# Attention with the transposes two steps and the value products three steps behind the scores, and the sink as a column of the score tile

## The chip, the cores and the metric

The kernel runs on 1 core of a Trainium2 chip. The metric is the device time of one execution in microseconds (us). The core's engines work in parallel, each on its own instruction queue: TensorE (PE, with its weight loads as PEld), VectorE (DVE), ScalarE (ACT), GpSimd (POOL) and SyncE (SP), which issues the loads of weights. They wait for each other by semaphores.

## The reference

Two blocks in a row on 512 tokens of width 1024. The first (a pooling mixer and a gated linear recurrence) isn't touched by the change. The second has two layers, each of this form:

```python
h = jnp.einsum('bsd,de->bse', x, w_in[l]) + b_in[l]
q, k, v, z_a, u_g, v_g, z_g, g_a, g_g = split_columns(h)
y_a = sliding_window_attention(q, k, v, attn_sinks[l]) * silu(z_a)
y_g = chunked_spatial_gating(gelu(u_g), gelu(v_g), ...) * silu(z_g)
merged = sigmoid(g_a) * (y_a @ w_branch_attn[l]) + sigmoid(g_g) * (y_g @ w_branch_gmlp[l])
x = layer_norm(ALPHA * x + merged @ w_out[l] + b_out[l], ln_g[l], ln_b[l])
...
# sliding_window_attention: 8 query heads, 2 key heads of 64, blocks of 128, window 128
scores = scores - slopes[:, :, None, None] * dist
scores = jnp.where(valid, scores, -jnp.inf)
m = jnp.maximum(scores.max(-1, keepdims=True), sink)
p = jnp.exp(scores - m)
denom = p.sum(-1, keepdims=True) + jnp.exp(sink - m)
out = (p / denom) @ v
```

A block of 128 queries sees its own block of 128 keys and the one before it. Block 0 sees only its own.

## The kernel before, in words

All matrix products with weights are made of three matmuls (`products`, L363 to L365): the weights and the activations are split into a part hi and a rest lo, and hi x hi, hi x lo and lo x hi are added up in PSUM. A *unit* is one output tile of 128 rows by 512 tokens: 8 contraction tiles of three matmuls, 24 in all. Its accumulator is `acc[0]` or `acc[1]` in turn, so a unit starts only when the result of the unit two before it has been evicted (`acc_done`).

The weights come in by SyncE to `raw`. In the second block VectorE makes `whi` of a piece (`c_split`, the CAST L1887) and GpSimd then makes `wlo` (`split_lo`, L358: `raw` less `whi`, both in SBUF), three units ahead of TensorE's use.

The order of the second block is written out in a list, `C_ORDER`. Its units are q0 to q3, k, v, za0 to za3, u0 to u3, vg0 to vg3 (one quarter of the contraction each, over all of `acc`), zg0 to zg3, ga0 to ga3, gg0 to gg3, then the branch products, and gates and branches again for the other half. Each engine walks this list; its part of an entry is its *slot*. ScalarE evicts a unit or makes its sigmoid or Gelu; for za and zg VectorE multiplies the sigmoid with the unit and so evicts it (L1896). After vg3 VectorE adds the bias (L1904), ScalarE does the Gelu (L1464), and VectorE takes mean and variance in the slot of zg0 (`vg_norm`, L1866 to L1873), of which ScalarE takes the root (L1467) before it makes the sigmoid of zg1. `vg_scale` (L1879) follows in the slot of zg1, and GpSimd multiplies and adds the norm's weights (L895, L897) behind its `split_lo` in four slots from zg3 on.

Hung to these units is the attention. A step is a head pair `p` and a block `b` of 128 queries, 16 steps a layer, one to each unit from za1 on (`side.append(("att", att))`). TensorE does its part of a step behind the unit, and VectorE and ScalarE behind the eviction. In slot s this happens:

- TensorE: scores of step s into the one bank `aux[:, 0]` (L1056, once the scores of step s-1 have been read), transposes of the probabilities of step s-1 (L1066), products with v of step s-2 (L1078).
- VectorE, `att_vector`: distance and mask added (L1814), maximum (L1818), maximum with the sink, its negation, and sink less maximum (L1821 to L1824). Then `c_split` of a weight piece. Then `att_vector_norm`: sum of exponentials and sink (L1832), reciprocal (L1834), scaling of the probabilities (L1837), and for the last block of a head pair the product of the output with za and its rest (L1842, L1845).
- ScalarE, `att_scalar`: the exponentials with their sum (L1376), exponential of the sink (L1379); then `att_scalar_turned`: the turned probabilities of step s-1 to SBUF (L1386), and the output's part hi (L1392).

The tiles `sc`, `pr`, `pt` and `sm` have two buffers each, by the step's parity.

## Time and profile before

| | before |
|---|---|
| time, median of 3 runs | 1731.24 us (1730.32 to 1731.7) |
| the profiled execution | 1731.74 us, span 1729.9 us |
| mean granted clock of TensorE | 0.987 of full |
| busy share of PE, DVE, ACT, POOL | 95%, 60%, 32%, 23% |
| attention of layer 0, first scores to last products | 1056.3 to 1196.4 us |
| the same of layer 1 | 1412.9 to 1554.1 us |

Times within the span count from its start. The durations used are those of the one profiled execution. An idle time is one of an engine between two of its instructions, put down to the instruction that ended it. Matmuls overlap their neighbours in the records, so the pace of TensorE is read from start to start.

### The profile page before, as it was taken

How to read it: one execution, taken by the hardware profiler on the slowest of the kernel's cores; microseconds unless marked ns; L12 is line 12 of the kernel's file. 1: busy time of each engine (PE TensorE's matmuls, PEld its weight loads, DVE VectorE, ACT ScalarE, POOL GpSimd, SP SyncE). 2: the span in 40 equal slices, each digit the busy share in tenths (PEclk: the TensorE clock that was granted, in tenths of full speed). 3: DMA queues.
4: the chain of work that ended last, by engine and by line, in shares of the span. 5: the costliest groups of instructions: out<-in, count | busy, mean ns of one | idle time of the engine just before them, and what ended most of it. 6: DMA issues, size and time to landing. Idle time of an engine off the chain costs nothing.

```text
span 1729.9 us, 31676 instructions
## 1 busy us (share of the span) xinstructions
PE 1643.8 (95%) x12890; PEld 1422.3 (82%) x12890; DVE 1042.3 (60%) x1636; ACT 555.5 (32%) x1000; POOL 393.1 (23%) x345
## 2 busy tenths in 40 slices
PE   7999899999999999999999799989999999989998
PEld 6999899988888888788887697757887887668876
DVE  6757475745765667476574366676525756664446
ACT  4323231333243232324323235453112235441121
POOL 0000000000422224042242123325350043253410
PEclk9999999999999999999999899999999999999999
DMA  3332223213212222221221132212223332222231
GB/s 128 98 94 89 67 96 98 93 55 103 74 51 74 75 68 81 73 65 60 74 75 62 49 121 86 73 49 98 73 98 122 112 92 71 73 66 81 98 122 49
DMA packets 112625, 142.23 MB, mean 82 GB/s; under 512 B 3068, under 2 KB 88480, under 8 KB 112480
## 3 DMA queue, kind: packets, MB, share of 16 engines
q1 hardware_dynamic: 108368, 133.07, 23.3%
q10 hardware_dynamic: 4032, 6.89, 1.3%
q8 instruction: 107, 1.75, 0.4%
q14 instruction: 38, 0.31, 0.1%
q0 software_dynamic: 80, 0.20, 0.0%
HBM read 137.01 MB, written 2.10 MB: 80 GB/s over the span
## 4 chain that ended last, share of the span: by engine, by line
PE 81%; DVE 11%; ACT 5%; issue 2%; DMA 0%; POOL 0%; DVEq 0%; SPq 0%; ACTq 0%; POOLq 0%
PE acc L363 23%; PE acc L365 22%; PE acc L364 22%; PE aux L517 2%; DVE sm L1832 1%; PE aux L363 1%; PE aux L365 1%; PE aux L364 1%; PE aux L534 1%; ACT pr L1376 1%; DVE ab L584 1%; PE aux L544 1%; PE aux L542 1%; DVE qb L573 1%; PE aux L503 1%
## 5 line engine op out<-in xcount | busy, mean ns | idle before, releaser
L363 PE MATMUL acc<-xhi,whi 128*128 128x264 f32 (+2 forms) x1888 | 632.4, 335 | 12.0 <-issue 4.4
L364 PE MATMUL acc<-xlo,whi 128*128 128x264 f32 (+2 forms) x1888 | 617.8, 327 | 0.0
L365 PE MATMUL acc<-xhi,wlo 128*128 128x264 f32 (+2 forms) x1888 | 617.5, 327 | 0.0
L363 PEld LDWEIGHTS acc<-xhi,whi 128*128 128x128 f32 x1888 | 357.0, 189 | 50.5 <-issue 13.0
L365 PEld LDWEIGHTS acc<-xhi,wlo 128*128 128x128 f32 x1888 | 357.4, 189 | 30.7
L364 PEld LDWEIGHTS acc<-xlo,whi 128*128 128x128 f32 x1888 | 357.6, 189 | 28.3 <-issue 0.9
L358 POOL TENSOR_TENSOR wlo<-raw,whi 128x1024 fp32r<-128x1024 f32 x84 | 205.0, 2441 | 352.5 <-DVE whi L1887 352.5
L354 ACT ACTIVATE whi<-raw 128x1024 fp32r<-128x1024 f32 x160 | 165.8, 1048 | 169.2 <-PE acc L365 156.7
L1680 DVE TENSOR_TENSOR wlo<-raw,whi 128x1024 fp32r<-128x1024 f32 x77 | 93.8, 1221 | 68.6 <-ACT whi L354 68.6
L358 DVE TENSOR_TENSOR wlo<-raw,whi 128x1024 fp32r<-128x1024 f32 x83 | 101.0, 1221 | 42.5 <-ACT whi L354 42.5
L1887 DVE CAST whi<-raw 128x1024 fp32r<-128x1024 f32 x84 | 65.7, 784 | 73.0 <-PE acc L365 73.0
L873 POOL TENSOR_TENSOR kb<-kb,tb 128x264 f32<-128x264 f32 (+1 forms) x96 | 85.5, 891 | 67.3 <-PE aux L517 36.0
L873 POOL TENSOR_TENSOR kb<-kb,fb 128x264 f32<-128x264 f32 x16 | 15.7, 980 | 363.4 <-PE aux L517 363.4
L859 POOL MEMSET ab<- 128x512 f32 x2 | 1.0, 526 | 375.1 <-DVE xlo L401 375.1
L363 PE MATMUL acc<-zhia,whi 128*128 128x264 f32 x256 | 73.6, 288 | 6.1 <-DVE zloa L1620 6.1
L573 DVE TENSOR_TENSOR qb<-qb,tb 128x256 f32<-128x256 f32 x96 | 64.9, 676 | 13.5 <-PE aux L517 8.9
L365 PE MATMUL acc<-zhia,wlo 128*128 128x264 f32 x256 | 72.7, 284 | 0.0
L364 PE MATMUL acc<-zloa,whi 128*128 128x264 f32 x256 | 72.6, 284 | 0.0
L1832 DVE TENSOR_TENSOR sm<-sm 128x2 f32<-128x2 f32 x32 | 58.1, 1816 | 21.3 <-ACT sm L1379 21.3
L1376 ACT ACTIVATE pr<-sc,sm 128x256 f32<-128x256 f32 (+1 forms) x64 | 30.4, 475 | 74.3 <-DVE sm L1824 74.3
L363 PEld LDWEIGHTS acc<-zhia,whi 128*128 128x128 f32 x256 | 48.1, 188 | 7.3 <-DVE zloa L1620 6.9
L1614 DVE TENSOR_TENSOR h<-acc,h 128x528 f32<-128x528 f32 x32 | 22.6, 708 | 51.0 <-PE acc L365 51.0
(282 smaller groups left out, 2755.6 us busy)
## 6 DMA issues: line engine op xcount, KB each, us to landing
raw<-in_w_in SPq DMA_DIRECT2D x38, 1024.0 KB, 5.1
raw<-in_hgrn_w_in SPq DMA_DIRECT2D x32, 1024.0 KB, 5.4
raw<-in_pool_w_in SPq DMA_DIRECT2D x16, 1024.0 KB, 5.2
raw<-in_pool_w_out SPq DMA_DIRECT2D x8, 1024.0 KB, 4.9
raw<-in_hgrn_w_out SPq DMA_DIRECT2D x8, 1024.0 KB, 5.0
raw<-in_w_out SPq DMA_DIRECT2D x8, 1024.0 KB, 4.9
raw<-in_pool_w_grp SPq DMA_DIRECT2D x4, 1024.0 KB, 5.3
raw<-in_w_branch_attn SPq DMA_DIRECT2D x4, 1024.0 KB, 5.0
```

The source lines that it names most:

```text
L354: act.activation(piece(whi, kind, m), raw_view(kind, m), ACT.Copy).then_inc(hi_ready, 1)
L358: dve.tensor_tensor(piece(wlo, kind, m), raw_view(kind, m), piece(whi, kind, m), ALU.subtract).then_inc(lo_ready, 1)
L363: pe.matmul(dst, stat[0], mov[0], start=first, stop=False)
L364: pe.matmul(dst, stat[0], mov[1], start=False, stop=False)
L365: return pe.matmul(dst, stat[1], mov[0], start=False, stop=last)
L517: mm = pe.matmul(dst, keys, q, start=True, stop=True)
L573: dve.tensor_tensor(second_halves(q, m), second_halves(q, m), blocks.unsqueeze(2).to_broadcast([P, CH * nb, m]), ALU.mult)\
L873: pool.tensor_tensor(first_halves(k, m), first_halves(k, m), both[:, :, 1].unsqueeze(2).to_broadcast([P, n, m]), ALU.mult)\
L1376: act.activation(pr[z][:, x, lo:], sc[z][:, x, lo:], ACT.Exp, bias=sm[z][:, 2, x:x + 1], accum_out=sm[z][:, 4, x:x + 1])\
L1680: dve.tensor_tensor(piece(wlo, kind, m), raw_view(kind, m), piece(whi, kind, m), ALU.subtract).then_inc(lo_ready, 1)
L1832: dve.tensor_tensor(sm[z][:, 6, :], sm[z][:, 4, :], sm[z][:, 5, :], ALU.add).then_inc(aprob, 1)
L1887: dve.tensor_copy(piece(whi, kind, M), raw_view(kind, M)).then_inc(hi_ready, 1)
```

## The change

The same work is put in another order and the sink is taken in otherwise. The transposes of a step stand two slots behind its scores, and the products with v three slots; the list gets one more slot for it (ga3). VectorE's sum, reciprocal and scaling move from behind the weight split of slot s to the start of the attention part of slot s+1 (in `att_vector`), ahead of the masking of step s+1's scores. The output of a head pair (`att_vector_out`) comes one slot later. ScalarE copies the turned probabilities ahead of the exponentials and no longer behind them. `sc` and `pr` get 257 columns, the last of which is the sink: it is copied in where a head pair begins (for either buffer), maximum, exponential and sum run over it, and so the separate operations on the sink fall out. The reduction gives the maximum negated.

```diff
-            sc = [sb(f"sc{s}", [P, 2, 2 * P], where=before_m) for s in range(2)]
-            pr = [sb(f"pr{s}", [P, 2, 2 * P], where=before_m) for s in range(2)]
+            sc = [sb(f"sc{s}", [P, 2, 2 * P + 1], where=before_m) for s in range(2)]
+            pr = [sb(f"pr{s}", [P, 2, 2 * P + 1], where=before_m) for s in range(2)]
...
-                    elif att < len(ATT) + 2 and att >= len(ATT):
+                    elif att < len(ATT) + 3 and att >= len(ATT):
...
-                if 1 <= s <= len(ATT):
-
-                    b = ATT[s - 1][1]
-                    pe.wait_ge(aprob, 4 * (base + s - 1) + 4)
-                    pe.wait_ge(apt_ready, 1 + base + s - 1)
+                if 2 <= s < len(ATT) + 2:
+
+                    t = s - 2
+                    b = ATT[t][1]
+                    pe.wait_ge(aprob, 3 * (base + t) + 3)
+                    pe.wait_ge(apt_ready, 1 + base + t)
                     for x in range(2):
                         for kb_ in range(0 if b else 1, 2):
                             mm = pe.transpose(aux2[:, 0, P * (2 * x + kb_):P * (2 * x + kb_ + 1)],
-                                              pr[(s - 1) % 2][:, x, P * kb_:P * kb_ + P], ident[:, :])
+                                              pr[t % 2][:, x, P * kb_:P * kb_ + P], ident[:, :])
                     mm.then_inc(apt_full, 1)
-                if 2 <= s:
-
-                    p, b = ATT[s - 2]
-                    pe.wait_ge(apt_ready, 1 + base + s - 1)
+                if 3 <= s:
+
+                    t = s - 3
+                    p, b = ATT[t]
+                    pe.wait_ge(apt_ready, 1 + base + t + 1)
                     if b == 0:
                         pe.wait_ge(ya_ready, 1 + 4 * i + p)
...
-                                           pt[(s - 2) % 2][:, 2 * x + kb_, :],
+                                           pt[t % 2][:, 2 * x + kb_, :],
...
             def att_scalar(i, s):
                 base = 16 * i
-                if s < len(ATT):
-                    p, b = ATT[s]
-                    lo, z = (0 if b else P), s % 2
-                    act.wait_ge(arow, 4 * (base + s) + 4)
-                    for x in range(2):
-                        act.activation(pr[z][:, x, lo:], sc[z][:, x, lo:], ACT.Exp,
-                                       bias=sm[z][:, 2, x:x + 1], accum_out=sm[z][:, 4, x:x + 1])\
-                           .then_inc(aexp, 1)
-                    act.activation(sm[z][:, 5, :], sm[z][:, 3, :], ACT.Exp).then_inc(aexp, 1)
-
-            def att_scalar_turned(i, s):
-                if 1 <= s <= len(ATT):
-                    b = ATT[s - 1][1]
-                    act.wait_ge(apt_full, 16 * i + s)
-                    z, first = (s - 1) % 2, (0 if b else 1)
+                if 2 <= s < len(ATT) + 2:
+                    t = s - 2
+                    z, first = t % 2, (0 if ATT[t][1] else 1)
+                    act.wait_ge(apt_full, base + t + 1)
                     act.activation(pt[z][:, :, :].rearrange("p (x k) q -> p x k q", x=2)[:, :, first:, :],
                                    aux2[:, 0, :].rearrange("p (x k q) -> p x k q", x=2, k=2)[:, :, first:, :],
                                    ACT.Copy).then_inc(apt_ready, 1)
-                if s >= 2 and ATT[s - 2][1] == CH - 1:
-                    p = ATT[s - 2][0]
+                if s < len(ATT):
+                    lo, z = (0 if ATT[s][1] else P), s % 2
+                    act.wait_ge(arow, base + s + 1)
+                    for x in range(2):
+                        act.activation(pr[z][:, x, lo:], sc[z][:, x, lo:], ACT.Exp,
+                                       bias=sm[z][:, 0, x:x + 1], accum_out=sm[z][:, 1, x:x + 1])\
+                           .then_inc(aexp, 1)
+                if s >= 3 and ATT[s - 3][1] == CH - 1:
+                    p = ATT[s - 3][0]
                     act.wait_ge(ya_ready, 1 + 4 * i + p + 1)
                     act.activation(yah[:, p, :], sq[p % 2][:, 0:SEQ], ACT.Copy).then_inc(yahi_ready, 1)
...
-                    for what, s in side:
-                        if what == "att":
-                            att_scalar_turned(i, s)
...
             def att_vector(i, s):
                 base = 16 * i
+                if 1 <= s < len(ATT) + 1:
+                    t = s - 1
+                    lo, z = (0 if ATT[t][1] else P), t % 2
+                    dve.wait_ge(aexp, 2 * (base + t) + 2)
+                    dve.reciprocal(sm[z][:, 2, :], sm[z][:, 1, :]).then_inc(aprob, 1)
+                    dve.wait_ge(aprob, 3 * (base + t) + 1)
+                    for x in range(2):
+                        dve.tensor_scalar(pr[z][:, x, lo:2 * P], pr[z][:, x, lo:2 * P], sm[z][:, 2, x:x + 1], None,
+                                          ALU.mult).then_inc(aprob, 1)
                 if s < len(ATT):
                     p, b = ATT[s]
                     lo, z = (0 if b else P), s % 2
+                    if b < 2:
+                        dve.tensor_copy(sc[z][:, :, 2 * P:2 * P + 1], sinks[:, 2 * p:2 * p + 2].unsqueeze(2))\
+                           .then_inc(sink_ready, 1)
                     dve.wait_ge(asc_full, base + s + 1)
                     for x in range(2):
-                        dve.scalar_tensor_tensor(out=sc[z][:, x, lo:], in0=nd[:, lo:], scalar=SLOPES[2 * p + x],
+                        dve.scalar_tensor_tensor(out=sc[z][:, x, lo:2 * P], in0=nd[:, lo:], scalar=SLOPES[2 * p + x],
                                                  in1=aux[:, 0, 2 * P * x + lo:2 * P * (x + 1)],
                                                  op0=ALU.mult, op1=ALU.add).then_inc(asc_ready, 1)
                     dve.wait_ge(asc_ready, 1 + 2 * (base + s) + 2)
-                    dve.tensor_reduce(sm[z][:, 0, :], sc[z][:, :, lo:], AX_X, ALU.max).then_inc(arow, 1)
-                    dve.wait_ge(arow, 4 * (base + s) + 1)
-                    sink = sinks[:, 2 * p:2 * p + 2]
-                    dve.tensor_tensor(sm[z][:, 1, :], sm[z][:, 0, :], sink, ALU.max).then_inc(arow, 1)
-                    dve.wait_ge(arow, 4 * (base + s) + 2)
-                    dve.tensor_scalar(sm[z][:, 2, :], sm[z][:, 1, :], -1.0, None, ALU.mult).then_inc(arow, 1)
-                    dve.tensor_tensor(sm[z][:, 3, :], sink, sm[z][:, 1, :], ALU.subtract).then_inc(arow, 1)
-
-            def att_vector_norm(i, s):
-                base = 16 * i
-                if s < len(ATT):
-                    p, b = ATT[s]
-                    lo, z = (0 if b else P), s % 2
-                    dve.wait_ge(aexp, 3 * (base + s) + 3)
-                    dve.tensor_tensor(sm[z][:, 6, :], sm[z][:, 4, :], sm[z][:, 5, :], ALU.add).then_inc(aprob, 1)
-                    dve.wait_ge(aprob, 4 * (base + s) + 1)
-                    dve.reciprocal(sm[z][:, 7, :], sm[z][:, 6, :]).then_inc(aprob, 1)
-                    dve.wait_ge(aprob, 4 * (base + s) + 2)
-                    for x in range(2):
-                        dve.tensor_scalar(pr[z][:, x, lo:], pr[z][:, x, lo:], sm[z][:, 7, x:x + 1], None,
-                                          ALU.mult).then_inc(aprob, 1)
-                if s >= 2 and ATT[s - 2][1] == CH - 1:
-                    p = ATT[s - 2][0]
-                    dve.wait_ge(ao_full, base + s - 1)
+                    dve.wait_ge(sink_ready, 8 * i + 2 * p + min(b, 1) + 1)
+                    dve.tensor_reduce(sm[z][:, 0, :], sc[z][:, :, lo:], AX_X, ALU.max, negate=True).then_inc(arow, 1)
+
+            def att_vector_out(i, s):
+                if s >= 3 and ATT[s - 3][1] == CH - 1:
+                    p = ATT[s - 3][0]
+                    dve.wait_ge(ao_full, 16 * i + s - 2)
                     dve.tensor_tensor(sq[p % 2][:, 0:SEQ], aux2[:, 1, :], za[:, p, :], ALU.mult)\
...
-                            att_vector_norm(i, s)
+                            att_vector_out(i, s)
```

VectorE behind unit zg0, from its eviction on (`sgc`: the sigmoid, `aux`: the scores). Before:

```order
L1896 SCALAR_TENSOR_TENSOR zg<-acc,vec,sgc 128x512 [waits sigc_ready]
L1814 SCALAR_TENSOR_TENSOR sc<-nd,aux 128x256 [waits asc_full]
...
L1818 TENSOR_REDUCE sm<-sc 128x2 [waits asc_ready]
...
L1887 CAST whi<-raw 128x1024 [waits lin_done,raw_landed0]
L1832 TENSOR_TENSOR sm<-sm 128x2 [waits aexp]
L1834 RECIPROCAL sm<-sm 128x2 [waits aprob]
L1837 TENSOR_SCALAR pr<-pr,sm 128x256 [waits aprob]
...
L1866 BN_STATS vgst<-vn 128x6 [waits vgg_ready] x4
```

Of the change, ahead of it the output of head pair 1 (`sqs`, `yal`):

```order
L1832 TENSOR_TENSOR sqs<-aux,za 128x512 [waits ao_full]
L1835 TENSOR_TENSOR yal<-sqs,yah 128x512 [waits yahi_ready]
L1886 SCALAR_TENSOR_TENSOR zg<-acc,vec,sgc 128x512 [waits sigc_ready]
L1808 RECIPROCAL sm<-sm 128x2 [waits aexp]
L1811 TENSOR_SCALAR pr<-pr,sm 128x256 [waits aprob]
...
L1821 SCALAR_TENSOR_TENSOR sc<-nd,aux 128x256 [waits asc_full]
...
L1826 TENSOR_REDUCE sm<-sc 128x2 [waits sink_ready,asc_ready]
L1877 CAST whi<-raw 128x1024 [waits lin_done,raw_landed0]
L1856 BN_STATS vgst<-vn 128x6 [waits vgg_ready] x4
```

The reciprocal and the scaling, which now are those of step 10, stand ahead of step 11's scores, and between the CAST and the statistics nothing is left.

TensorE behind unit zg1, where step 12 (a block 0) has its scores. The number behind `pr` and `pt` is the buffer, which is the parity of the step. Before:

```order
L1056 MATMUL aux<-kc1,qc 128x2x128 [waits asc_ready]
L1066 MATMUL aux2<-ident,pr1 128x128 [waits apt_ready,aprob]
L1066 MATMUL aux2<-ident,pr1 128x128 x3
L1078 MATMUL aux2<-pt0,vtc 64x128 [waits apt_ready]
L1078 MATMUL aux2<-pt0,vtc 64x128 x3
```

Of the change:

```order
L1056 MATMUL aux<-kc1,qc 128x2x128 [waits asc_ready]
L1067 MATMUL aux2<-ident,pr0 128x128 [waits apt_ready,aprob]
L1067 MATMUL aux2<-ident,pr0 128x128 x3
L1080 MATMUL aux2<-pt1,vtc 64x128 [waits apt_ready]
L1080 MATMUL aux2<-pt1,vtc 64x128 x3
```

The kinds and numbers of matmuls are the same. The transposes took step 11 and now take step 10, the products took step 10 and now take step 9.

## Rows read from the trace of the kernel before

**Rows 1.** The waits of TensorE (PE), 1050 to 1580 us: idle us, times, longest.

```profile
PE aux L1066 <- DVE pr L1837: 20.3, 9, 4.0
PE acc L363 <- ACT ug L1438: 2.4, 2, 1.2
...
PE acc L363 <- DVE vn L1904: 2.0, 2, 1.0
PE aux L1056 <- DVE sc L1814: 0.6, 1, 0.6
```

**Rows 2.** Stretches: length, busy us (count) of PE, PEld, DVE, ACT, POOL; granted clock, DMA share, GB/s.

```profile
1145.90:1152.00 6.10, 3.60 (x23) 2.76 (x23) 5.44 (x12) 1.65 (x2) 1.69 (x1) 1.00 0.51 168
1157.00:1165.00 8.00, 4.46 (x19) 3.20 (x19) 7.39 (x17) 4.65 (x9) 2.34 (x1) 0.79 0.00 0
1502.50:1509.10 6.60, 4.09 (x19) 2.97 (x18) 5.88 (x14) 1.68 (x2) 1.73 (x1) 0.74 0.49 159
1514.30:1521.00 6.70, 3.81 (x23) 2.86 (x23) 6.32 (x12) 3.98 (x7) 2.26 (x1) 1.00 0.00 0
1533.20:1543.20 10.00, 6.05 (x22) 4.52 (x22) 9.11 (x14) 6.17 (x10) 7.25 (x5) 0.66 0.00 0
```

**Rows 3.** TensorE in order of time: start us, us, engine, line, operation.

```profile
1070.65 0.50 PE L363 MATMUL acc<-xhi,whi 128*128 128x512 f32 x1
...
1076.22 1.02 PE L1056 MATMUL aux<-kc,qc 128*128 128x512 f32 x2
1077.08 0.60 PE L1066 MATMUL aux<-ident,pr 128*128 128x128 f32 x4
1077.61 0.66 PE L1078 MATMUL aux<-pt,vtc 128*64 128x128 f32 x8
1078.20 0.50 PE L363 MATMUL acc<-xhi,whi 128*128 128x512 f32 x1
...
1128.85 1.02 PE L1056 MATMUL aux<-kc,qc 128*128 128x512 f32 x2
...
1182.10 0.80 PE L363 MATMUL acc<-xhi,whi 128*128 128x512 f32 x1
```

**Rows 4.** The chain that ended last, 1130 to 1190 us: start us, us, what.

```profile
1130.35 2.48 DVE vn L1904 x4
...
1133.52 0.70 DVE sm L1818
...
1136.45 1.28 ACT L1464
...
1143.42 0.70 DVE sm L1818
1144.60 1.09 ACT pr L1376 x4
...
1148.46 2.39 DVE vgst L1866 x4
...
1155.61 0.40 DVE sc L1814 x2
...
1160.67 1.82 DVE vn L1879 x4
...
1169.57 0.63 ACT yah L1392
...
1178.12 2.47 DVE pr L1837 x2
```

**Rows 5.** VectorE and GpSimd in order of time, 1144.3 to 1147.8 us.

```profile
1144.48 0.69 DVE L1887 CAST whi<-raw 128x1024 fp32r<-128x1024 f32 x1
...
1145.25 2.34 POOL L358 TENSOR_TENSOR wlo<-raw,whi 128x1024 fp32r<-128x1024 f32 x1 [7.50 <-DVE whi L1887]
...
1145.82 1.79 DVE L1832 TENSOR_TENSOR sm<-sm 128x2 f32<-128x2 f32 x1 [0.65 <-ACT sm L1379]
...
1147.64 0.17 DVE L1834 RECIPROCAL sm<-sm 128x2 f32<-128x2 f32 x1
```

More of the change, by code:

```diff
@@ L307, in program @@
         asc_full, asc_ready, arow = sem("asc_full"), sem("asc_ready"), sem("arow")
-        aexp, aprob = sem("aexp"), sem("aprob")
+        aexp, aprob, sink_ready = sem("aexp"), sem("aprob"), sem("sink_ready")
         apt_full, apt_ready, ao_full = sem("apt_full"), sem("apt_ready"), sem("ao_full")
```

## The prediction

> **What bounds the kernel now.** I read the waits of TensorE in the attention stretch of either layer first, then small stretches of the span around its longest idles, the chain that ended last through the same stretch, TensorE's own rows in order of time, and last what VectorE and GpSimd do there. "Step s" is one of the 16 attention steps of a layer (head pair s//4, block s%4). It hangs on one unit of the projection: za1 to za3 carry steps 0 to 2, u 3 to 6, vg 7 to 10, zg 11 to 14, ga0 step 15.
>
> The reader is to see in [rows 1] that TensorE idles 25.3 us in the attention of the two layers (20.3 + 2.4 + 2.0 + 0.6), and that 20.3 of them stand before the transposes L1066, which want the probabilities that VectorE normalises at L1837. In [rows 2] the longest idles show as a stretch less the busy time in it: 2.50 and 3.54 us in layer 0 (and one more like the second, from 1177 on), 2.51, 2.89 and 3.95 us in layer 1. Behind four of these six the granted clock is at half, the lower of its two levels of 1.2 and 2.4 GHz, for some us. What the mean of a stretch lacks to 1.00, times its length, is lost: 8.0 x 0.21 = 1.7 us twice, 6.6 x 0.26 = 1.7 us and 10.0 x 0.34 = 3.4 us, 8.5 us together. So attention costs TensorE 25.3 + 8.5 = 33.8 us beyond its work. The work itself runs at a fixed pace [rows 3]: a unit takes 5.57 us (1070.65 to 1076.22), a full step 0.86 us for scores, 0.53 for four transposes and 0.59 for eight products (1.98 in all), and a block 0 half of each.
>
> Why VectorE is late is in [rows 4]. From 1130.35 to 1180.59 the chain that ended last runs over VectorE and ScalarE alone: bias adds of vg (L1904), step 10, Gelu (L1464), sigmoid and eviction of zg0, step 11, statistics (L1866), root, sigmoid and eviction of zg1, step 12, and so on. Each attention step in it holds scores, maximum, exponentials, sum, reciprocal and scaling end to end, since the engines do all of step s inside one unit. [rows 5] shows its worst link: a 128x2 addition of 1.79 us (L1832), where the reciprocal of the same size, with one input, takes 0.17. It begins at 1145.82 while GpSimd's L358 runs (1145.25 + 2.34 = 1147.59) and ends at 1147.61. So the addition waits for GpSimd, whose operation the CAST just ahead sets going. The Trainium skill says why (SBUF — State Buffer, Who interferes with whom): VectorE shares a pair of ports with GpSimd under an exclusive lock, and an instruction with two SBUF inputs needs it against a GpSimd instruction that reads SBUF. The trace agrees by these rows.
>
> **The change, part by part.**
>
> *The order of the steps.* The exponentials of step s are scaled at the start of VectorE's next slot, transposed by TensorE two slots after the scores, and multiplied with v three slots after. TensorE's share of work is the same: 0. What was waited for inside one slot, exponentials 1.1 us, addition 1.8, reciprocal and scaling 0.85 (1147.61 to 1148.46), now has a slot of 7.55 us (1070.65 to 1078.20) before its transposes. That covers it even if the scaling waits out one GpSimd operation. All idles before L1066 go.
>
> *The output of a head pair* (L1842, L1392, L1845) comes a slot later. Before, that of pair 0 stood in front of the eviction of u3, and that of pair 1 in front of the bias adds of vg. These are the idles of 2.4 and 2.0 us over both layers in [rows 1]; both go. Pair 1 now stands between the exponentials of step 10 and the Gelus.
>
> *What is still late.* The chain through the statistics stays, so I walk it again in the new order, in layer 0. TensorE ends unit vg3 at 1128.85 - 1.2 = 1127.65, and the adds start there, at 1127.8. Before, the chain from their start (1130.35) to the masked scores of step 12 (1155.61 + 0.40 = 1156.01) took 25.66 us [rows 4]. Now:
> - Up to the Gelus 0.8 comes in (scaling of step 9 ahead of step 10), and CAST, product and copy of pair 1 (0.69 + 0.62, a quarter of the adds, + 0.63 = 1.94) replace the small operations, exponentials and copy between the end of the maximum, 1134.22, and 1136.45 (2.23): + 0.5.
> - Between the end of the maximum of step 11 (1144.12) and the statistics (1148.46), of 4.34 only the CAST of 0.69 is left: - 3.65.
> - Ahead of the scores of steps 11 and 12 the scaling of the step before comes in, 0.8 twice, and the copy of the sink once. No row shows that copy. It is worth 0.17 by a 128x2 operation that meets nobody and 2.47 by the two scalings that met GpSimd [rows 4, 5]; here GpSimd has been done for 5 us, so I take 0.17. Together + 1.8.
>
> 25.66 + 0.5 - 3.65 + 1.8 = 24.3, so the scores of step 12 are masked at 1152.1, and only then may TensorE write those of step 13 into the same bank. TensorE would be there, with 1.7, 1.7 and 1.55 for steps 10, 11 and 12 and three units, at 1127.65 + 4.95 + 3 x 5.57 = 1149.3. **One idle of 2.8 us is left per layer**, before L1056 in place of L1066.
>
> *From there on* TensorE goes 1152.1 + 1.98 + 5.57 = 1159.65, + 1.7 + 5.57 = 1166.9, + 1.7 = 1168.6 for the start of ga1, where before it stood at 1182.10 [rows 3]: 13.5 us earlier. VectorE must have step 13 masked by 1159.65. After the CAST of that slot, about 1153.3, the four scalings of vn wait for GpSimd's operation until 1155.7 and take 1.8; then come the eviction (0.6, as one of the adds of the same width), the scaling of step 12 (0.8) and the scores (0.8, twice those of a block 0): 1159.7. So there is no slack at this place, and I put 0.4 us per layer on it; its bounds are 0 and the 2.4 us of one GpSimd operation. In ga1 and ga2 the scalings of steps 14 and 15 lie behind GpSimd's work on vn, and may be held up again; they took 2.47 us before [rows 4], and now have until the end of the next unit.
>
> *Small operations.* The sink as column 257 takes an addition, a negation, a subtraction, a maximum and an exponential from each of 32 steps, and gives 16 copies and one column more. After the shift none of them is on TensorE's path, save those in the walk: 0. Without that cover the addition alone would be worth 1.79 us a step.
>
> **Sum.** 33.8 - 2 x 2.8 = 28.2. The idle that is left may bring the clock down: of the three idles nearest its size (2.50, 2.51, 2.89) one did, for 1.7 us, so 2 x 0.57 = 1.1. With 2 x 0.4 for the tight place, 28.2 - 1.1 - 0.8 = 26.3. The profiled execution took 1731.74 us (span 1729.9), 0.5 above the median of the runs shown, so 1731.2 - 26.3 = 1704.9, say **1705**. Nothing later takes it back by the rows: the gate units and the rest of the layer follow at TensorE's pace, and the earlier they start, the earlier all feeds are asked for.
>
> **Rivals.**
>
> *The GpSimd lock moves on (0.22).* The addition that took the wait is gone, but the scaling L1837 took 2.47 us in place of some 0.65 where it met GpSimd [rows 4, 5], and so can the four scalings of vn and the CAST. If two such meetings a layer fall on the tight place or on the chain, and each idle brings the clock down, that is 4 x 0.8 to 4 x 2.0 us and 2 x 1.1 for the clock: 1710 to 1716 (three in four of GpSimd's 2.34 us at the most). For it: no slack at step 13. Against: each scaling now has a slot to itself. By the skill's section named above, a copy, cast or scalar operation in a mode that uses both ports takes the lock as well, and who begins first keeps it; with this the scalings of vn would wait as I assumed, or hold GpSimd up instead, which none waits for so soon.
>
> *The chain is shorter than the walk (0.07).* Gelus and sigmoids get ahead, TensorE isn't held before step 13, or for less than 1 us: 1731.2 - 33.8 + 0 to 3.5 = 1697 to 1701.
>
> *The shift does little (0.05).* The bound is the chain through the statistics and not the step inside one slot. Then the 3.65 us a layer fall out, at most with the 4.4 us before vg and zg and 1.7 of the clock, and the other idles move to L1056: 1731.2 less 7.3 to 13.4, 1718 to 1724. Against: the chain has its three engines in series only where one slot holds a whole step, and that is what is undone.
>
> *Slower (0.03).* The copy of the turned probabilities (L1386 before) now stands ahead of the exponentials on ScalarE and waits for transposes that TensorE issues behind the scores of the same slot. So ScalarE, VectorE and TensorE form a ring over two slots: transposes 0.53, copy 0.6, table 1.3, exponentials 1.1, scaling 0.85, and 2.3 for GpSimd, 6.7 us. It decides only if it outgrows the two slots of 15 us that it has. It would have to add more than 26.5 / 32 = 0.8 us to every step; at 1 us it gives 1737.
>
> **How the numbers follow.** My forecast has 0.63, with its own range of 1702 to 1709 (the tight place at 0 to 1.5 us per layer, the clock down at neither or both idles). With the lock rival up to 1714 and the upper part of the shorter chain, 1700 to 1714 leaves out less than 2 in 10. A measurement tells 0.2%, about 3.5 us, from no change: faster 0.95, same 0.02, slower 0.03.
>
> **What would show it.** In the profile after: no idle before the transposes over 0.5 us; no idle before the first unit of vg or of zg; one wait per layer of L1056 for the scores of step 12, 2 to 3 us, within the zg units; the scaling at 0.6 us in the zg slots and up to 2.5 in the ga slots; the next units at full clock or one stretch at half; ga1 some 13.5 us earlier in layer 0. I am wrong if the waits on VectorE within zg add up to over 5 us a layer, or if a new one stands before the products or the scores of the u and za slots.

## The result, and the profile after

| | before | after |
|---|---|---|
| time, median | 1731.41 us (4 runs, 1730.32 to 1731.7) | 1701.99 us (4 runs, 1698.48 to 1704.31) |
| ratio, 95% interval | | 0.9826 [0.9813, 0.9839] |
| the profiled execution | 1731.74 us, span 1729.9 us | 1704.31 us, span 1702.5 us |
| mean granted clock of TensorE | 0.987 | 0.988 |

The kernel became 29.4 us faster, 1.7%. The forecast was 1705 us with a range of 1700 to 1714.

The waits of TensorE in the attention of both layers, 1050 to 1570 us, of the kernel after (idle us in total, how many times, the longest):

```profile
PE aux L1056 <- DVE sc L1821: 4.1, 2, 2.1
PE acc L363 <- issue: 2.1, 1, 2.1
PE acc L363 <- DVE xlo L1710: 0.6, 1, 0.6
```

Against [rows 1], the line of the transposes (20.3 us, nine times), and those before the first unit of vg (2.4) and of zg (2.0), are gone. What is left are two waits, one per layer, of the scores of step 13 for the masking of step 12 (L1821). The last two lines stand outside attention, and were there before. The two waits as stretches of the span, and the first 200 us of attention (length, busy us with counts of PE, PEld, DVE, ACT, POOL, granted clock, DMA share, GB/s):

```profile
1148.50:1154.50 6.00, 3.92 (x16) 2.20 (x16) 5.76 (x11) 5.26 (x11) 2.58 (x1) 0.72 0.12 43
1491.90:1497.90 6.00, 3.93 (x18) 2.61 (x18) 5.78 (x11) 5.26 (x11) 2.60 (x1) 0.80 0.12 41
1050.00:1250.00 200.00, 197.78 (x947) 155.07 (x946) 115.87 (x202) 83.48 (x146) 84.09 (x38) 0.99 0.23 76
```

TensorE idles 6.00 - 3.92 = 2.08 us and 2.07 us. What the clock lacks to 1.00 costs 6.0 x 0.28 = 1.7 us and 6.0 x 0.20 = 1.2 us more. In the same 200 us of the kernel before, TensorE was busy for 10.6 us less, and VectorE for 15.2 us more:

```profile
1050.00:1250.00 200.00, 187.22 (x889) 145.01 (x887) 131.04 (x249) 81.34 (x158) 75.30 (x35) 0.98 0.21 69
```

The chain that ended last in the kernel after, in order of time. It answers to [rows 4]:

```profile
1126.82 2.48 DVE vn L1894 x4
...
1133.29 1.28 ACT L1459
1134.59 2.19 ACT vn L1459 x4
...
1138.09 0.70 ACT sgc L1434
1138.82 0.75 DVE zg L1886
...
1141.59 0.68 DVE whi L1877
1142.28 2.39 DVE vgst L1856 x4
...
1147.94 0.70 ACT rstd L1434
1148.66 0.75 DVE zg L1886
1149.52 0.62 DVE pr L1811 x2
1150.32 0.29 DVE sc L1821
1150.66 2.06 PE aux L1056 x2
```

The statistics (`vgst`) now follow the CAST (`whi`) directly. Before, 4.34 us lay between the maximum and the statistics. After the scores at 1150.66 the chain runs over TensorE without a break, where before it stayed on VectorE and ScalarE until 1180.59. Over the whole span TensorE holds 86% of the chain.

### The profile page after: what moved, and what is told of

Its sections match the earlier page's. It is cut to its first block, busy times and chain, and to the rows that moved or that the text cites. A ratio compares the mean times of both kernels' runs of the same rounds, so it can differ in the third digit from the quotient of the medians.

```text
span 1702.5 us, 31564 instructions
## 1 busy us (share of the span) xinstructions
PE 1638.4 (96%) x12890; PEld 1421.3 (83%) x12890; DVE 996.3 (59%) x1524; ACT 554.5 (33%) x968; POOL 396.0 (23%) x345
## 4 chain that ended last, share of the span: by engine, by line
PE 86%; DVE 7%; ACT 3%; issue 2%; DMA 0%; DVEq 0%; POOL 0%; SPq 0%; ACTq 0%; POOLq 0%
PE acc L363 25%; PE acc L365 23%; PE acc L364 23%; PE aux L517 2%; PE aux L1056 1%; PE aux L363 1%; PE aux L364 1%; PE aux L365 1%; PE aux L534 1%; DVE ab L584 1%; PE aux L1080 1%; PE aux L503 1%; PE aux L544 1%; PE aux L542 1%; DVE qb L573 1%
## 5 line engine op out<-in xcount | busy, mean ns | idle before, releaser
L517 PEld LDWEIGHTS aux<-qb,kb 128*32 128x32 f32 x3072 | 32.6, 111 | 23.6 <-issue 8.1
L876 POOL TENSOR_TENSOR tb<-tb 128x132 f32<-128x132 f32 (+5 forms) x96 | 52.3, 545 | 0.0
```

The source lines that it names most:

```text
L517: mm = pe.matmul(dst, keys, q, start=True, stop=True)
L876: pool.tensor_tensor(tb[x][2 * m][:, 0:n], both[:, :, 0], both[:, :, 1], ALU.mult)\
```

## The experiments

They ran in three groups, each beside the kernel before on one chip. In the profile of that kernel the waits for VectorE in attention are 22.9 us, and 2.4 more are for ScalarE [rows 1]. Its medians were 1732.27 us (beside the new order alone, the column alone, the CAST behind the scaling and the output alone), 1731.34 us (beside the column with the CAST, and the products with the output) and 1730.08 us (beside the last four of the table). Gains are against these.

| kernel | median us (range) | ratio, 95% interval | waits for VectorE within attention, us |
|---|---|---|---|
| the new order alone | 1704.75 (1704.27 to 1705.81) | 0.9843 [0.9826, 0.9859] | 6.8 |
| the sink's column alone | 1714.50 (1707.9 to 1715.06) | 0.9888 [0.9864, 0.9913] | 10.8 |
| CAST behind the scaling | 1716.02 (1713.31 to 1717.55) | 0.9903 [0.9887, 0.992] | 13.1 |
| column, and CAST behind the scaling | 1706.48 (1704.39 to 1708.63) | 0.9857 [0.9837, 0.9877] | 7.5 |
| output alone later | 1766.93 (1764.75 to 1771.17) | 1.0204 [1.018, 1.0227] | 54.6 |
| products and output later | 1732.38 (1727.98 to 1736.71) | 1.0007 [0.9995, 1.002] | 23.8 |
| the kernel after again | 1702.03 (1699.53 to 1705.87) | 0.9843 [0.9828, 0.9858] | 4.2 |
| two banks for the scores | 1697.75 (1693.83 to 1698.99) | 0.9803 [0.9787, 0.982] | 1.5 |
| statistics first | 1696.58 (1695.44 to 1698.3) | 0.9802 [0.9789, 0.9816] | none |
| both of these | 1694.82 (1694.5 to 1697.95) | 0.9797 [0.9783, 0.9811] | none |

### The new order alone

The kernel after, with the tiles 256 wide and the five operations on the sink as before. The sum with the sink now stands at the start of the next slot:

```diff
-                    dve.reciprocal(sm[z][:, 2, :], sm[z][:, 1, :]).then_inc(aprob, 1)
+                    dve.tensor_tensor(sm[z][:, 6, :], sm[z][:, 4, :], sm[z][:, 5, :], ALU.add).then_inc(aprob, 1)
...
+                    dve.reciprocal(sm[z][:, 7, :], sm[z][:, 6, :]).then_inc(aprob, 1)
```

> The new order of the steps alone: transposes two and products three steps behind, scaling at the start of the next slot, but the sink handled as before (maximum, negation, subtraction, exponential and the 128x2 addition stay, 256 columns). Theory A, that what cost TensorE was the whole step standing in one slot: nearly all of the gain is here. The chain through the statistics gets the small operations back, 0.4 us ahead of the split of step 11 and some 0.2 us for each of three additions, so the wait for the scores of step 12 grows from 2.1 to about 3.1 us a layer, and the time is 1703 to 1708 us. Theory B, that the 1.8 us addition with two SBUF inputs was what cost, and the sink column did the work: it still waits for GpSimd in every slot, and the time is 1715 us or more.

Measured: 27.5 us faster than before. The order carries nearly all of the gain. Its waits:

```profile
PE aux L1056 <- DVE sc L1821: 6.5, 4, 2.8
...
PE aux L1080 <- DVE sqs L1837: 0.3, 1, 0.3
```

They are 2.7 us longer in all than those of the kernel after. The medians, each against its own runs of before, lie 1.9 us apart (27.5 against 29.4), and the intervals of the ratios overlap. The waiting addition is still there: it takes 903 ns in the mean in the attention of layer 0, against 1817 before, since in its new place it often finds GpSimd idle. No transposes wait for it. The order consists of several moves (the scaling, the transposes, the products, the output, ScalarE's copy), and this run does not tell what each is worth.

### The sink's column alone

The kernel before, with 257 columns, the copy of the sink, the negated reduction and the reciprocal straight from the sum of the exponentials; every step stays in its slot.

```diff
-                    dve.tensor_tensor(sm[z][:, 6, :], sm[z][:, 4, :], sm[z][:, 5, :], ALU.add).then_inc(aprob, 1)
...
-                    dve.reciprocal(sm[z][:, 7, :], sm[z][:, 6, :]).then_inc(aprob, 1)
+                    dve.reciprocal(sm[z][:, 2, :], sm[z][:, 1, :]).then_inc(aprob, 1)
```

> The sink as column 257 alone, in the order of before (everything of a step in one slot, transposes one step behind). Theory A: the wait for GpSimd passes from the addition to the scaling, which then takes 1.5 to 2.2 us for its pair in place of 0.6. A step in the chain gets 0.5 to 0.7 us shorter (small operations ahead of the exponentials, and the split's start 0.37 earlier), which over five or six steps of the chain a layer makes 1722 to 1727 us. Theory B: the lock took only the addition; the scaling stays at 0.6 us, each step gets over 2 us shorter and the time is 1705 to 1713 us.

Measured: 17.8 us faster. What stands behind the exponentials, on VectorE, in this kernel:

```profile
1133.93 0.17 DVE L1829 RECIPROCAL sm<-sm 128x2 f32<-128x2 f32 x1 [0.63 <-ACT pr L1376]
1134.13 2.06 DVE L1832 TENSOR_SCALAR pr<-pr,sm 128x256 f32<-128x256 f32 x2
```

and on GpSimd:

```profile
1133.38 2.39 POOL L358 TENSOR_TENSOR wlo<-raw,whi 128x1024 fp32r<-128x1024 f32 x1 [6.86 <-DVE whi L1882]
```

GpSimd ends at 1135.77, and the pair of scalings at 1136.19. So the wait of the addition has passed to the scaling, as expected. But the stretch from the eviction of zg0 to the statistics still became 0.9 us shorter (6.41 to 5.51), where 0.5 to 0.7 was expected, and the time is 7.5 us below the lowest that this theory expected (1722), and above the 1705 to 1713 of the other: a miss in size. The waits before L1066 fell from 20.3 to 9.4 us. A likely reason, argued and not tried by itself, is that a lateness is carried from slot to slot, so that a little less in each adds up.

### The CAST behind the scaling

The kernel before, with the CAST (and so GpSimd's operation) after the normalisation of the same slot.

```diff
+                    for what, s in side:
+                        if what == "att":
+                            att_vector_norm(i, s)
                     if (kind != "k4" or half == 1) and PIECES <= M < WO_PIECE:
                         c_split(C_PIECES * i + M)
                     for what, s in side:
                         if what == "att":
-                            att_vector_norm(i, s)
+                            att_vector_out(i, s)
```

> The kernel before with one thing moved: VectorE makes the hi part of the weights (the CAST) behind the scaling of the probabilities and not ahead of the addition, so GpSimd has no work of its own while the addition runs. Theory A (the addition waits for GpSimd, whose work this CAST releases): it takes 0.16 to 0.2 us and no longer 1.8; TensorE gets its transposes 1.6 us sooner in each of the waits, less 0.7 us for the CAST where the chain goes on over VectorE: 1716 to 1724 us. Rival C (the addition is long for another reason, such as the arrival of ScalarE's sums): it stays at 1.8 us and the time at 1731 us or above.

Measured: 16.3 us faster. The addition and the reciprocal of [rows 5] with the scaling behind them, now with GpSimd done long before:

```profile
1145.04 0.16 DVE L1832 TENSOR_TENSOR sm<-sm 128x2 f32<-128x2 f32 x1 [1.25 <-ACT sm L1379]
1145.24 0.17 DVE L1834 RECIPROCAL sm<-sm 128x2 f32<-128x2 f32 x1
1145.44 0.62 DVE L1837 TENSOR_SCALAR pr<-pr,sm 128x256 f32<-128x256 f32 x2
1145.97 0.69 DVE L1890 CAST whi<-raw 128x1024 fp32r<-128x1024 f32 x1
```

The addition takes 0.16 us in place of 1.79 in a kernel that differs in this order alone. So its time before was a wait for GpSimd. To undo this wait, at the price of the CAST's 0.69 us behind the scaling, is worth 16 us in the old order.

### Column and CAST together, in the old order

The edits of the last two, on the kernel before: no operation waits for GpSimd behind the exponentials, the small operations are gone, every step stays in its slot.

> The kernel before with the sink column and with the split behind the scaling: the old order without the 128x2 addition, without the small operations ahead of the exponentials and without GpSimd at work while the scaling runs, which then takes 0.6 us. Theory A (a whole step in one slot costs by itself): the waits for the transposes shrink but stay, some 3 to 8 us over both layers, and those before vg and zg partly too: 1706 to 1712 us. Theory B (the lock and the small operations were all of it, and the new order is worth nothing beyond): 1702 us or less, as the changed kernel.

Measured: 24.9 us faster, at the edge of what Theory A expected (1706 to 1712 us). The scaling takes 367 ns in the mean in the attention of layer 0, against 1125 with the column alone, and the waits for VectorE fall from 22.9 us [rows 1] to 7.5, among them:

```profile
PE aux L1066 <- DVE pr L1832: 3.3, 5, 1.0
...
PE acc L363 <- DVE vn L1902: 0.6, 2, 0.3
```

The second line is all that is left of the 4.4 us before the first units of vg and zg, with the output in its old place. So a shorter step nearly removes those idles by itself. The new order (27.5), and a shorter step in the old order (24.9), are two ways to nearly the same gain. Such gains don't add up: the order and the column together give 29.4, and not 27.5 + 17.8 = 45.3.

### The output alone later, and the products with it

The first kernel moves the output of a head pair one slot on (the list gets one more slot for it), and nothing else. The second moves the value products as well.

```diff
-                if s >= 2 and ATT[s - 2][1] == CH - 1:
-                    p = ATT[s - 2][0]
-                    dve.wait_ge(ao_full, base + s - 1)
+                if s >= 3 and ATT[s - 3][1] == CH - 1:
+                    p = ATT[s - 3][0]
+                    dve.wait_ge(ao_full, base + s - 2)
```

> The kernel before with one thing moved: the output of a head pair (product with za, hi and rest) one slot later, as in the change, at the price of one more slot. Theory A: the idles before the first unit of vg (1.2 us) and of zg (1.0 us) go in both layers, but pair 1 now stands between step 10 and the Gelus and gives most of the second back: 1726 to 1729.5 us. Rival D: the waits on VectorE behind it take all of it: 1730 to 1732 us.

Measured: 34.7 us slower, far outside of what either side expected. Its waits, over its longer attention (1050 to 1620 us):

```profile
PE aux L1078 <- DVE sqs L1842: 44.8, 6, 8.5
PE aux L1066 <- DVE pr L1837: 9.4, 4, 3.5
```

The instruction that waits, in its timeline:

```profile
1104.16 0.68 DVE L1842 TENSOR_TENSOR sqs<-aux,za 128x512 f32<-128x512 f32 x1
...
1104.99 0.69 PE L1078 MATMUL aux<-pt,vtc 128*64 128x128 f32 x4 [6.17 <-DVE sqs L1842]
```

The products of step 4, 8 and 12 open a new head pair in the bank that holds the output of the pair before. With the output a slot later, they want it read in the very slot in which VectorE reads it last, behind the masking and the normalisation with the addition that waits for GpSimd. TensorE stands still for the whole of that, three times a layer. My expectation had followed only what comes behind the output on VectorE, not who waits for the bank. To see whether this is the whole cause, the second kernel moves the products too, so that the output stands to them as before:

```diff
-                if 2 <= s:
+                if 3 <= s:
...
-                    p, b = ATT[s - 2]
-                    pe.wait_ge(apt_ready, 1 + base + s - 1)
+                    p, b = ATT[s - 3]
+                    pe.wait_ge(apt_ready, 1 + base + s - 2)
```

> The kernel before with the products with v and the output of a head pair both one slot later (the transposes stay one step behind). The run with the output alone moved had the products of a block 0 waiting in the same slot for the output of the pair before, 44.8 us in all; here that distance is as it was. Theory A, as for that run: the idles before the first unit of vg and of zg go, 2.2 us a layer, pair 1's output (1.9 us) now lies ahead of the Gelus in the chain that bounds zg, and the scalings stay late: 1725 to 1730 us. If it stays above 1740 us, the 44.8 us had another cause.

Measured: no difference from before. The loss is undone, so the bank was its cause. The idles before vg and zg are gone, as meant, but nothing is gained, as the rival had it. The two lines of waits for VectorE in this kernel:

```profile
PE aux L1066 <- DVE pr L1839: 21.0, 9, 4.4
PE aux L1056 <- DVE sc L1816: 2.8, 2, 1.4
```

23.8 us, where [rows 1] had 25.3 (2.4 of them for ScalarE). The 4.4 us before the two units went over to the scores (0.6 to 2.8) and the transposes (20.3 to 21.0), and 1.5 vanished, too little to be seen in the time. One more wait had to come in with this edit: the turned probabilities have two buffers, so ScalarE copies those of step s-1 only when the products of step s-3, now in the same slot, are done. It held ScalarE once in each layer, in layer 0 for 3.5 us in slot 16 (ga1), and there ScalarE idled another 5.8 us for TensorE behind it, so it doesn't look as if it hid a gain.

### What is left in the kernel after: two banks, the statistics first, both

The repetition of the kernel after in the same group:

> The changed kernel unaltered, on one chip with the three that follow, so that differences of a few us between them can be told. 1698 to 1705 us by its four runs so far; the spread follows the granted clock behind the idle that is left.

It came out at the same time, 1702.03 us against 1701.99.

Scores in the two banks `aux[:, 0]` and `aux[:, 1]` in turn:

```diff
-                    pe.wait_ge(asc_ready, 1 + 2 * (base + s))
+                    pe.wait_ge(asc_ready, 1 + 2 * (base + s) - (2 if s else 0))
...
-                    pe.matmul(aux[:, 0, :].rearrange("p (x k) -> p x k", x=2)[:, :, lo:],
+                    pe.matmul(aux[:, s % 2, :].rearrange("p (x k) -> p x k", x=2)[:, :, lo:],
```

> The changed kernel with the scores of even and odd steps in two banks (aux[:, 0] and aux[:, 1]), so TensorE may write step 13's scores before step 12's have been read. Theory E (the idle before step 13 comes from the one bank alone): the whole 2.1 us per layer go, with the half clock behind them: 1694 to 1697 us. Theory A (VectorE's chain is late, the bank only decides what waits for it): the idle moves to the transposes of step 11, whose scaling VectorE ends 0.1 us before step 12's masking, and shrinks only by the 0.9 us of the scores that now go ahead: 1697 to 1701 us.

Measured: 4.3 us below the repetition. The wait of the scores is gone, and a shorter one before the transposes of the same slot is left of it:

```profile
1151.00 0.66 PE L1067 MATMUL aux<-ident,pr 128*128 128x128 f32 x4 [0.77 <-DVE pr L1811]
```

So the bank alone did not make the idle: VectorE was late, as Theory A had it, with 0.8 us left in each layer where it had 1.2.

The statistics of vg at the head of VectorE's slot of zg0, ahead of the eviction and of step 11:

```diff
+                    if stage == "zg" and n == 0:
+                        vg_norm(i)
                     if stage in ("za", "zg"):
```

> The changed kernel with the statistics of vg at the head of VectorE's slot of zg0 (into its 3.8 us of idling while ScalarE makes the Gelus) and not behind the attention step and the split. Theory A (the idle left is the chain Gelu, sigmoid, step 11, statistics, root, sigmoid, step 12): the root is ready with ScalarE's exponentials of step 11, the sigmoid of zg1 comes about 2 us sooner and the idle before step 13 falls from 2.1 to at most 0.5 us per layer, with no half clock behind it: 1695 to 1699 us. Theory F (step 11 itself or zg0's sigmoid holds it, the statistics only follow): 0.6 us of the idle or less is gained, 1700 us or above.

Measured: 5.5 us below the repetition, and no wait for VectorE or ScalarE is left in attention. The statistics and the sigmoid's eviction of zg1, which stood at 1142.28 and 1148.66 in the kernel after:

```profile
1134.29 2.47 DVE L1856 BATCH_NORM_STATS2 vgst<-vn 128x6 f32<-128x512 f32 x4 [0.22 <-ACT vn L1459]
...
1145.93 0.75 DVE L1888 SCALAR_TENSOR_TENSOR zg<-acc,vec,rstd 128x512 f32<-128x512 f32 x1 [4.08 <-ACT rstd L1434]
```

They come 8.0 and 2.7 us earlier. This execution was about 1.0 us ahead already at the CAST of the slot before (1130.36 against 1131.33), so the move itself brings 7.0 and 1.8, the latter as expected. In the kernel after VectorE idled at this place for the sigmoid of zg0 (3.79 us), so the statistics cost little there, and the chain through the root is off the end.

> Both edits together: two banks and the statistics first. Theory A: nothing is left for the second bank to do once the chain is short, so it equals the kernel with the statistics first within 1 us, 1695 to 1699 us. If the two gains are of different waits, it is 2 us or more below each.

Measured: 1694.82 us, the lowest median of all, and lower than both measurements of the kernel after: 36.6 us below the first measurement of before and 35.3 below that of its own group. It is 1.8 us below the statistics first alone, where at most 1 was expected, but their ranges overlap, so whether the banks add anything once the statistics are first stays open. The profile of the statistics first shows no wait that they could still remove.

## Why the prediction was right, point by point

- **All idles before the transposes go**: right. Not one of the nine is left, and with the old sink operations (the new order alone) none comes back either.
- **The idles before vg and zg go**: right as to what is seen. But the reason given, the later output, holds only together with the rest. Alone it costs 34.7 us, and with the products it gives nothing. I had counted the 4.4 us as a gain of this step. With the rest of the old order they only move. They go where VectorE's step is no longer late: in the new order, and, down to 0.6 us, with the column and the CAST moved, where the output stays in its place.
- **One idle of 2.8 us per layer before L1056, for the masking of step 12**: right in place, number and cause; 2.08 and 2.07 us in size. It is smaller because the chain from the adds to the masked scores took 1150.6 - 1126.8 = 23.8 us, not 24.3, and because the profile counts less idle than the pace does: by its pace TensorE was held back from 1148.4 on (2.3 us), by the profile's idle from 1148.6. One term was missing in the walk besides. The transposes and products that were put off have not been done when TensorE reaches the scores of step 10: two transposes of step 8 (a block 0) and eight products of step 7, 0.31 + 0.59 = 0.90 us. The scores of step 10 began at 1126.62 and the adds at 1126.82, not at 1127.65 and 1127.8. This brings the adds and TensorE's arrival (1148.4 and not 1149.3) forward alike, by some 1 us, so it cancels out of the idle.
- **The clock comes down at one of two idles, 1.1 us**: too small in both traces. In the profiled execution it came down at both, for 1.7 + 1.2 = 2.9, and in the profile of the repetition at one, for 6.0 x 0.28 = 1.7. Other executions had a higher mean clock (up to 0.993 against 0.988), but where they kept it no trace shows.
- **The tight place at step 13, 0.8 us**: it cost nothing. VectorE does there:

```profile
1151.57 3.94 DVE L1869 TENSOR_SCALAR vn<-vn,vgst,vgr 128x512 f32<-128x512 f32 x4
1155.44 0.74 DVE L1886 SCALAR_TENSOR_TENSOR zg<-acc,vec,sgc 128x512 f32<-128x512 f32 x1
1156.10 0.15 DVE L1808 RECIPROCAL sm<-sm 128x2 f32<-128x2 f32 x1
1156.28 0.48 DVE L1811 TENSOR_SCALAR pr<-pr,sm 128x128 f32<-128x128 f32 x2
1156.68 0.16 DVE L1817 COPY sc<-sinks 128x2 f32<-128x2 f32 x1
1156.75 0.75 DVE L1821 SCALAR_TENSOR_TENSOR sc<-nd,aux 128x256 f32<-128x256 f32 x2
```

  The four scalings of `vn` did wait for GpSimd (its operation ran from 1151.74 for 2.58 us), as the walk had it. The end, though, is 1157.5 where 1159.7 was forecast, because the slot began earlier (masked at 1150.6 and not at 1152.1) and the scaling is that of a block 0. TensorE came at 1159.96, so 2.5 us of slack were there. Some 1.7 of them come from the half clock behind the idle: at its full pace TensorE would have come at 1150.66 + 1.98 + 5.57 = 1158.2 by the walk's figures, and 0.7 us of slack would be left.
- **ga1 in layer 0 starts 13.5 us earlier**: 1169.05 against 1182.10 [rows 3], 13.05 us. The forecast was 1168.6. This near hit is in part luck: the walk had the scores of step 13 start 1.4 us too late, and had left the 1.7 us of the half clock behind them out of this place.
- **The small operations are worth nothing after the shift**: by the waits 2.7 us over both layers, by the times 1.9 with overlapping intervals. In the old order they would have been worth 17.8 us together with the addition that waits for GpSimd, which I had put at 1.79 a step.
- **The sum**: the idles and the clock that are left give 4.15 + 2.9 = 7.05 us in place of 5.6 + 1.1 + 0.8 = 7.5. So 33.8 - 7.05 = 26.75 should have been gained between the profiled executions, and 27.4 was (1731.74 to 1704.31). That the total is so near is partly luck: the idles came out 1.45 us smaller and the tight place 0.8, the clock 1.8 larger. By the medians the gain is 29.4 us, 3.1 more than forecast; the profiled execution of the kernel after was the slowest of its four. Two slips in the prediction's text, 26.5 for 26.3 in the slower rival and 1716 for 1715 as the upper end of the lock rival, change nothing.

**The lock rival** was right in its mechanism and not in its price. The groups of VectorE in the attention of layer 0 (1050 to 1200 us), before:

```profile
L1832 DVE TENSOR_TENSOR sm<-sm 128x2 f32<-128x2 f32 x16 | 29.1, 1817 | 10.7 <-ACT sm L1379 10.7
L1837 DVE TENSOR_SCALAR pr<-pr,sm 128x256 f32<-128x256 f32 (+1 forms) x32 | 13.1, 451 | 0.6
...
L1845 DVE TENSOR_TENSOR yal<-sqs,yah 128x512 fp32r<-128x512 f32 x4 | 2.8, 693 | 2.8 <-ACT yah L1392 2.8
```

and after:

```profile
L1811 DVE TENSOR_SCALAR pr<-pr,sm 128x256 f32<-128x256 f32 (+1 forms) x32 | 20.3, 674 | 0.6
...
L1835 DVE TENSOR_TENSOR yal<-sqs,yah 128x512 fp32r<-128x512 f32 x4 | 6.5, 1632 | 3.0 <-ACT yah L1390 3.0
```

The addition's 29.1 us are gone. Of them 7.2 come back at the scaling, 3.7 at `yal`, and 2.0 at the four scalings of `vn` (1.9 to 3.9), which the walk had foreseen. In the zg slots, where the end was at stake, the scaling took 0.62 us. It took 2.56 and 3.16 us in the ga slots, where the next transposes are a unit away. So these waits lie where TensorE does not wait for them. The rule of the Trainium skill that I had weighed (SBUF — State Buffer, Who interferes with whom), that a scalar operation in a mode with both ports is locked out too, agrees with the 2.06 us of the scaling in the kernel with the column alone. In which mode the scaling ran, the trace does not show.

**The shift does little**, **shorter chain** and **the ring on ScalarE** did not happen: 27.5 us came with the shift alone, the waits of 2.1 us stand in both layers, and no wait of TensorE for ScalarE is left within attention.

## What to carry to other kernels

When small late waits stand in many slots of one stage, look for the link that they share, here one operation held by GpSimd in each step, and for the slot in which a whole dependent chain is squeezed. Here the new order alone gave 27.5 us, the shorter step alone (column and CAST) 24.9, and the column added about 2 to the new order where it gave 17.8 in the old, so the gains of such cures must not be added. When a reader of a buffer is moved to a later slot, list its next writer first: the output moved by itself cost more than the whole change brought. And what is put off makes an engine arrive earlier at the places ahead of it. Here that moved both ends of the idle by some 1 us and so left its size alone, but a walk along the chain should start from the new time of arrival, since it need not cancel elsewhere.

## What the runs showed of the hardware

- **The same idle halves the clock or doesn't.** Stretches of the repetition of the kernel after, one for each layer:

```profile
1146.80:1152.80 6.00, 3.91 (x16) 2.08 (x16) 5.73 (x11) 5.27 (x10) 2.58 (x1) 0.72 0.17 58
1488.00:1500.00 12.00, 9.92 (x49) 7.38 (x48) 9.59 (x23) 8.57 (x13) 2.63 (x1) 1.00 0.25 83
```

  TensorE idles 2.09 and 2.08 us at the same point of the program. In layer 0 the clock falls to 0.72 in the mean of the stretch; in layer 1 it stays at full. In the first profile it fell in both layers. What decides it is not shown. Runs of the kernel after lie up to 6 us apart, and the mean clock goes with it: 1704.31 us at 0.988 and 1698.48 us at 0.993. So the idles cost more than their length in some runs, and 4.2 us of them, once removed by the statistics ahead, gave 5.5 by the medians.
- **A pair of scalings of 128x256 with one tile as input waits for GpSimd** (2.06 us in place of 0.62), and so do the four of 128x512 on `vn` (3.94 in place of 1.82). Both follow the CAST that sets GpSimd going: with the CAST moved behind the scaling and nothing else changed, the scaling's mean fell from 1125 to 367 ns in the kernels with the column, and the four on `vn`, which then stand right behind the CAST, rose from 1.91 to 3.96 us in those without it. A reciprocal of 128x2 takes 0.17 us whether GpSimd runs (1133.93, with the column alone) or not (1145.24, with the CAST behind the scaling).
- **The copy of the sink** (128x2) took 0.16 us each time it is shown here, with GpSimd idle (1156.68, where GpSimd had ended at 1154.32).
